# One 4 MB weight unit near the end: sixteen-way transfer against a 64-row piece and eight 8-row pieces

## The reference

```python
N_EXPERTS, TOP_K, D_FF = 32, 4, 1024
logits = (u @ w_router + b_router)
top_vals, top_idx = lax.top_k(logits, TOP_K)
top_w = jax.nn.softmax(top_vals)
...
hb = swiglu_clamped(u[tok] @ w1[e] + b1[e])     # w1[e]: 1024 x 2048
yb = (hb @ w2[e] + b2[e]) * wt[:, None]         # w2[e]: 1024 x 1024
```

## Time and profile before

| | |
|---|---|
| median of 3 runs | 1384.36 us (1383.05 to 1388.33) |
| the profiled execution, its own time | 1384.41 us |
| its span, first to last instruction | 1382.5 us |
| TensorE busy with matmuls | 1304.3 us, 94% of the span |
| mean granted TensorE clock | 0.984 |
| transferred | 469.28 MB, 339 GB/s over the span |

### The profile page before, as it was taken

One profiled execution on the slowest core, in us unless ns is written; L12 is line 12 of the kernel. 1 busy time (PEld: TensorE's weight loads), 2 busy tenths in 40 slices (PEclk: granted clock), 3 DMA queues, 4 the chain that ended last, 5 costly groups with the idle time before them and its releaser, 6 DMA issues.

```text
span 1382.5 us, 18188 instructions
## 1 busy us (share of the span) xinstructions
PE 1304.3 (94%) x7377; PEld 685.1 (50%) x7377; DVE 383.0 (28%) x947; ACT 278.4 (20%) x635; POOL 24.2 (2%) x40
## 2 busy tenths in 40 slices
PE   9999999999999999999999899899899999899897
PEld 5677887556885544443443343333333333333332
DVE  1056476676131611211121112111112211112112
ACT  3136334374001311111111111111111111111111
POOL 3000000000000000000000000000000000000000
PEclk9999999999999999999999999999999999999999
DMA  8744433345957699999999999999999999999994
GB/s 275 235 130 128 152 123 122 116 127 172 321 192 304 259 420 421 429 432 430 429 431 432 429 431 429 432 430 427 434 427 436 426 430 433 429 432 430 430 425 187
DMA packets 62543, 469.28 MB, mean 339 GB/s; under 512 B 3605, under 2 KB 36649, under 8 KB 48220
## 3 DMA queue, kind: packets, MB, share of 16 engines
q1 hardware_dynamic: 59068, 457.89, 81.2%
q0 software_dynamic: 1952, 5.61, 1.4%
q10 hardware_dynamic: 1440, 4.52, 0.9%
HBM read 466.61 MB, written 1.13 MB: 338 GB/s over the span
## 4 chain that ended last, share of the span: by engine, by line
PE 70%; DMA 25%; DVE 2%; issue 2%; ACT 1%; DVEq 0%; POOL 0%; SPq 0%
PE bank L1340 67%; DMA ring<-in_w 20%; DMA arena<-in_w 6%; PE bank L1802 1%; PE bank L1750 1%; PE bank L1458 0%; ACT arena L650 0%; PE bank L1382 0%; PE bank L1645 0%; PE bank L1460 0%; DVE arena L981 0%; DVE arena L1331 0%; DVE ring L1017 0%; ACT wdt L841 0%; PE bank L1528 0%
## 5 line engine op out<-in xcount | busy, mean ns | idle before, releaser
L1340 PE MATMUL bank<-ring,arena 128*64 128x512 f32 (+1 forms) x2024 | 503.3, 604 | 29.6 <-DMA ring<-in_w 23.2
L1340 PE MATMUL bank<-arena 128*128 128x64 bf16 (+6 forms) x3162 | 404.2, 382 | 36.1 <-DMA arena<-in_w 19.2
L1340 PEld LDWEIGHTS bank<-ring,arena 128*64 128x64 f32 (+1 forms) x2024 | 191.8, 144 | 306.4 <-issue 264.1
L1340 PEld LDWEIGHTS bank<-arena 128*128 128x128 bf16 (+3 forms) x3162 | 183.2, 122 | 268.4 <-issue 227.5
L1340 PE MATMUL bank<-arena,ring 128*128 128x256 f32 (+4 forms) x1408 | 283.2, 379 | 1.5 <-ACT ring L672 1.5
L1340 PEld LDWEIGHTS bank<-arena,ring 128*128 128x128 f32 (+1 forms) x1408 | 229.9, 180 | 46.8 <-issue 4.5
L1251 DVE TENSOR_SCALAR arena<-bank 128x256 f32<-128x256 f32 x64 | 27.1, 423 | 689.7 <-PE bank L1340 689.7
L845 ACT ACTIVATE arena<-arena 128x256 f32<-128x256 f32 x64 | 26.7, 417 | 454.1 <-DVE arena L1251 454.1
L1340 PE MATMUL bank<-arena,wdt 64*128 64x512 f32 (+1 forms) x280 | 69.4, 602 | 0.7 <-ACT arena L854 0.7
L854 ACT ACTIVATE arena<-bank 128x512 f32<-128x512 f32 x32 | 19.1, 597 | 221.0 <-PE bank L1340 221.0
L845 ACT ACT_TABLE_LOAD x31 | 39.8, 1283 | 0.6
(11 more groups left out here) (249 smaller groups left out, 584.3 us busy)
## 6 DMA issues: line engine op xcount, KB each, us to landing
ring<-in_w SPq DMA_DIRECT2D x48, 4096.0 KB, 39.5
arena<-in_w SPq DMA_DIRECT2D x34, 4096.0 KB, 39.1
ring<-in_w SPq DMA_DIRECT2D x18, 2048.0 KB, 15.7
ring<-in_w_in SPq DMA_DIRECT2D x34, 1024.0 KB, 5.7
arena<-in_w SPq DMA_DIRECT2D x9, 2048.0 KB, 10.0
ring<-in_w_ssm SPq DMA_DIRECT2D x8, 1024.0 KB, 8.5
ring<-in_w_att SPq DMA_DIRECT2D x16, 256.0 KB, 7.1
ring<-in_w_out SPq DMA_DIRECT2D x4, 1024.0 KB, 5.0
```

Of the source, the lines that this page charges most:

```text
L1340: return tn.matmul(o, lhsT, rhs, start=first, stop=last, skip_group_check=True)
```

## The change

One unit of the stream, number 85, is fetched in another form. Ahead of the change it is one transfer of 128 rows. After it, SP issues a transfer of rows 0 to 63 and then eight transfers of eight rows each, for rows 64 to 127. The first adds to the place's own semaphore as before, the eight add to a new semaphore. TensorE waits for both before it reads the unit. The bytes, their places in SBUF and all other transfers are the same.

```diff
-        LAST_UNITS = UNITS - 4
+        LAST_UNITS, SPREAD_UNIT = UNITS - 4, 85
...
+            def half_of_unit(u, used):
+
+                sp.wait_ge(slot_used, used)
+                dst, src = places[u % PLACES], unit_source(u)
+                sp.dma_start(dst[0:P // 2, :], src[0:P // 2, :]).then_inc(place_loaded[u % PLACES], 16)
+                for r in range(P // 2, P, 8):
+                    sp.dma_start(dst[r:r + 8, :], src[r:r + 8, :]).then_inc(spread_loaded, 16)
...
             for u in range(2 * PLACES + rounds * ROUND, LAST_UNITS):
-                unit(u, u // 3, free_at(u))
+                if u == SPREAD_UNIT:
+                    half_of_unit(u, free_at(u))
+                else:
+                    unit(u, u // 3, free_at(u))
...
             def unit_arrived(u, rounds=0):
 
                 pe.wait_ge(place_loaded[u % PLACES], rounds * 16 * 3 + 16 * (u // PLACES) + 16)
+                if u == SPREAD_UNIT:
+                    pe.wait_ge(spread_loaded, 16 * (P // 2 // 8))
```

More of the change, by code:

```diff
@@ L267, in hybrid_layer @@
                              "esig_ready", "hs_ready", "hT_ready", "hT_saved"))
-        b_ready, gw_ready, ye_saved, last_sc_ready, fin_ready = (sem(n) for n in (
-            "b_ready", "gw_ready", "ye_saved", "last_sc_ready", "fin_ready"))
+        b_ready, gw_ready, spread_loaded, ye_saved, last_sc_ready, fin_ready = (sem(n) for n in (
+            "b_ready", "gw_ready", "spread_loaded", "ye_saved", "last_sc_ready", "fin_ready"))
         def cols_of(w, c0, kt=KT, k0=0, n=256):
```

## The result

The changed kernel takes 1426.48 us (median of 4, 1423.25 to 1431.0), the one before 1384.24 us (median of 4, 1383.05 to 1388.33) in the same comparison. The ratio is 1.0306, with a 95% interval of 1.0287 to 1.0325: slower by 42 us. The forecast was 1380.0 us in a range of 1378.0 to 1389.5; it was wrong in sign and in size, and the time is outside the range.

What follows compares the result with a forecast made beforehand. The prediction took DMA and TensorE as near their limit, with unit 91's landing deciding the end. 1384.4 - 4.9 for earlier arrivals + 0.5 for a possible slower clock gave 1380.0 us, range 1378 to 1389.5.

Steps and rivals of the forecast that it cites:

- What bounds the kernel: Whole span: DMA and TensorE near their limit; unit 91's landing decides, with the end 55.0 us behind it.
- The clock's price of a long wait: TensorE's matmuls behind a weight wait of 2.5 us or more: a slower clock costs 1.5 us beyond the wait.
- Two groups of engines 10 us apart: End of the weight stream: eight DMA engines finish some 10 us behind the other eight, so units arrive by the late half.
- the fetch of instructions: Likely source of the late half: 71 packets of 16 KB, 8 us each on eight engines; an inference outside the sum.
- the first of the part by part: Unit 85's 64-row transfer: spread over all sixteen engines, four rows each.
- the price of 1.22 us a row: DMA packets: one row of 32 KB takes one engine 1.22 us, at 26.9 GB/s.
- gaps between them: Unit 85's small transfers: gaps taken as nothing; at a tenth of a us each, 0.8 us on the half ahead.
- a gain of 4.9 us: Landings from unit 85 to 91: the late half carries four rows fewer, so units arrive 4.9 us earlier.
- Which engines get the extra rows: Unit 85's eight-row pieces: all on the same eight engines, taken as the half ahead, about three to one.
- rival 1: Unit 85's extra rows hit the late half: landings 4.9 us later, 1389.3 us or up to 1391; chance 0.20.
- SP's issues, the wait on TensorE: Nine issues at 0.33 us, 2.7 us more, push nothing behind them; TensorE's second wait costs nothing.
- Rival 3: Unit 85's small pieces pile on one or two engines: 1447 us on one, 1408 on two; chance 0.03.

Runs made afterwards that it cites:

- both sides apart: Changed kernel with each eight-row piece of unit 85 taking every fourth row, in SBUF and in memory: 1412.13 us, ratio 1.021.
- the column halves: Changed kernel with unit 85 as two transfers of all 128 rows, each with half of the columns: 1384.75 us, ratio 1.0006.
- the rows apart: Changed kernel with unit 85's even rows in one transfer and its odd rows in eight pieces of eight: 1397.81 us, ratio 1.0102.
- the mirror: Changed kernel with sides swapped: rows 64 to 127 in one transfer, rows 0 to 63 in eight pieces of eight: 1412.03 us.
- the row halves at the early unit: Kernel before the change with only unit 9, not unit 85, fetched as two transfers of 64 rows: 1395.89 us.

## Why the prediction was wrong, step by step

**What bounds the kernel: right.** DMA and TensorE are both near their limit, unit 91's landing sets the end, and a delay of the stream goes into the time one for one: unit 91 lands 38.2 us later, the span grows by 39.8 us. The clock's price of a long wait, 1.5 us, was 1.7 us behind unit 91. That "each wait of 2.5 us or more" costs it was too strong: behind the 2.54 us with both sides apart it was nothing.

**Two groups of engines 10 us apart: right** in the main (by the increments the last of each group are 8.5 us apart at unit 85, 10.1 at unit 91), and it seems to matter in a way that wasn't seen: the two halves cost 12.3 us where the groups are close and 22.6 us where they are apart. The cause that the prediction names, the fetch of instructions, no run tested.

**The step that failed** is the first of the part by part: "The 64-row transfer: spread over all sixteen engines as the 128 rows are, it is four rows each", and with it the price of 1.22 us a row for any row. The count of rows was right and the price wasn't. A row takes 1.21 to 1.22 us in the 128-row transfers and in alternate rows. In 64 neighbouring rows it takes 2.56 us, in a piece of eight neighbours about 4.5 us. The bound above nothing for the small transfers, 0.8 us in all for "gaps between them", looked for the cost in the count of transfers, which the column halves show to be nothing, and not in where they land. No row of the trace before shows a transfer of fewer than 128 rows inside the stream, so both ends of that cost were taken from 128-row ones. In place of a gain of 4.9 us, 33.5 us of stream were lost.

The loss by its terms: 33.5 us of stream lost between 1245 and 1310, of which two row halves alone are some 21 (the nine windows of that run from 1245 to 1290 sum to 2035 of 3870, 21.3 us; its unit 91 lands 18.4 us later by its last increment and 20.7 us by its first, so the windows are good to some 3 us). The pieces of neighbours would be the rest, some 12 us. Then 4.9 us for the two engines that end last. 33.5 + 4.9 = 38.4, against 38.2 at unit 91, and the increments give the same split, 33.2 and 4.9.

**Which engines get the extra rows: right for six of eight.** The share at the end has no half left and two engines late, and the increments of unit 91 show two, twelve and two. The prediction called its choice a guess, at three to one, so the six are luck. With the rows apart there are two late ones again, so without the slow writes the sum would have come out at +4.9 and not -4.9 (an estimate; no run has the one without the other): the end waits for the latest engine, and two late engines are enough. That the trade takes whole groups was wrong, and rival 1 holds for those two.

The Trainium skill's rule in DMA: Bandwidth & Descriptors, Why a DMA increments its semaphore by 16, by which a transfer of eight rows takes the lowest eight engines, fits the times of pieces alone (12.55 and 22.6 us for eight and sixteen). No run names the engines. The Trainium skill's advice in Rules for kernel authors of the same page, against two transfers to halves of the partitions, is right for halves of neighbours, and they cost 12 to 23 us here, where the prediction took it to leave 1384.4. The reason that it gives, the same engines for both, isn't what the runs show: two transfers of alternate rows cost nothing.

**SP's issues, the wait on TensorE: right**, nothing lost there. **Rival 3** had the nearest time (1408 to 1447) and the wrong reason: the pieces weren't on one or two engines, but on eight, which wrote into the same few partitions. It got 3 in 100.

**Open.** While only one group of eight passes the halves, all sixteen engines are at half rate (the two row halves: 177 to 216 GB/s at a full share from 1250 to 1285, and no row under 2.35 us). If only engines with rows of the halves were held up, the other group should have gone on at full rate for part of that. Which rows of a 64-row transfer go to which engine, and whether one jam holds up the others on its way, no view shows. Also open is why the mirror costs 28 us and the change 42 us.

No version here beats the kernel before. Two sets of alternate rows and the column halves equal it (ratios 1.0004 and 1.0006); next come the row halves at the early unit, 0.9% slower, and the pieces of alternate rows, 1.0%.

## What to carry to other kernels

A DMA is priced by where its rows land as well as by its bytes and engines: neighbouring partitions share a way into SBUF, so a transfer over 64 of them takes as long as one over 128 (12.7 and 12.3 us), and two such halves nearly twice as long (22.75 us). If a large load has to be cut, cut it by columns, or by alternate rows; both cost nothing here. A share of busy DMA engines near 1 with GB/s down by half was the mark of it here, and units already under way paid for it too. Before work is moved from late engines to early ones, find out that every one of the receivers is early: one late one sets the end.

## What the runs showed of the hardware that was not expected

- 96 and 112 neighbouring rows take longer than 128: 16.9 and 16.5 us against 12.3.
- One pair of 64-row transfers in a full stream slows the rows of other units too: of 214 rows in 35 us none took under 2.35 us, where 1.22 is usual. It lasts 22 us at half rate where the engines were close, 40 us where they were some 10 us apart.
- Sixty-four rows taken alternately run at full rate (7.6 us with the fixed part), sixty-four neighbours at half (12.7 us); the source, apart or not, makes no difference (6.15 and 6.3 us for a piece alone).
